# Two pairs' gate products computed beside the first token half, 19 pairs in place of 18, and another order in the first out stage

## The reference

```
for l in range(2):
    h = rms_norm(x, norm_gains[l, 0]);  z = h @ w_in[l]
    y_main = pool_mixer(...) if l == 0 else dilated_mixer(...)
    y = concatenate([y_main, memory_attn(...)]) @ w_out[l]      # "out"
    x = x + rms_norm(y, norm_gains[l, 1])
    h = rms_norm(x, norm_gains[l, 2])
    gu = h @ w_gate_up[l]                                       # "ffn", "st"
    y = (silu(gu[..., :2816]) * gu[..., 2816:]) @ w_down[l]     # "down"
    x = x + rms_norm(y, norm_gains[l, 3])
```

## Time and profile before

| what | before |
|---|---|
| median of three runs | 2039.13 us (2037.52 to 2039.89) |
| profiled execution, its own time | 2038.86 us |
| its span in the profile | 2037.2 us |
| mean granted clock of PE | 0.996 |
| PE busy | 1989.5 us, 98% |
| DVE busy | 1429.8 us, 70% |
| ACT busy | 894.0 us, 44% |
| POOL busy | 315.4 us, 15% |

### The profile page before, as it was taken

The page is one execution under the profiler, slowest core; times in us unless marked ns, Lnnn a source line. Parts: engine busy times, 40 slices in busy tenths (PEclk is TensorE's granted clock), DMA queues, the critical chain, the costliest instruction groups (busy, mean ns, idle before and its releaser), DMA issues.

```text
span 2037.2 us, 25039 instructions
## 1 busy us (share of the span) xinstructions
PE 1989.5 (98%) x9470; PEld 1597.3 (78%) x9470; DVE 1429.8 (70%) x1861; ACT 894.0 (44%) x1481; POOL 315.4 (15%) x177
## 2 busy tenths in 40 slices
PE   8999999999999999999999999999999999999997
PEld 6776878888888878888777776688788888888886
DVE  6567686576788875666445467677789988875665
ACT  6446353445545354343444456836522222234341
POOL 3645000111211000000000001210224323300001
PEclk9999999999999999999999999999999999999999
DMA  5228841456688877666222222152256644476644
GB/s 178 101 73 301 301 140 47 160 207 217 231 295 306 299 263 242 209 236 229 83 83 83 83 67 59 43 179 85 96 196 230 226 177 165 174 294 248 221 153 162
DMA packets 122199, 363.64 MB, mean 178 GB/s; under 512 B 11616, under 2 KB 13024, under 8 KB 116832
## 3 DMA queue, kind: packets, MB, share of 16 engines
q1 hardware_dynamic: 105616, 331.89, 46.2%
q10 hardware_dynamic: 16464, 30.15, 4.3%
HBM read 241.28 MB, written 114.43 MB: 175 GB/s over the span
## 4 chain that ended last, share of the span: by engine, by line
PE 46%; DVE 4%; issue 2%; ACT 2%; DMA 2%; POOL 0%; SPq 0%; POOLq 0%; ACTq 0%; DVEq 0%
PE PS L1013 5%; PE PS L1014 5%; PE PS L1015 5%; PE PS L750 5%; PE PS L755 5%; PE PS L751 5%; PE PS L1031 3%; PE PS L1032 3%; PE PS L1033 3%; PE PSC L886 2%; PE PTR L916 2%; PE PX L903 2%; DMA inner<-TP 1%; DVE SS L1884 0%; DVE CL L2138 0%
## 5 line engine op out<-in xcount | busy, mean ns | idle before, releaser
L1031 PE MATMUL PS<-RP,DH 128*128 128x512 f32 x616 | 240.6, 391 | 3.0 <-DVE RP L2320 3.0
L1033 PE MATMUL PS<-RP,DL 128*128 128x512 f32 x616 | 239.8, 389 | 0.0
L1032 PE MATMUL PS<-RP,DH 128*128 128x512 f32 x616 | 239.7, 389 | 0.0
L1013 PE MATMUL PS<-BHT,SH 128*128 128x512 f32 x576 | 224.1, 389 | 0.0
L1014 PE MATMUL PS<-BLT,SH 128*128 128x512 f32 x576 | 224.1, 389 | 0.0
L1015 PE MATMUL PS<-BHT,SL 128*128 128x512 f32 x576 | 224.1, 389 | 0.0
L2771 POOL TENSOR_TENSOR WL<-WR,WH 128x1024 fp32r<-128x1024 f32 (+2 forms) x40 | 84.1, 2117 | 677.0 <-ACT WH L1178 669.5
L1013 PE MATMUL PS<-BH,SH 128*128 128x512 f32 x432 | 168.3, 389 | 1.6 <-DVE TP L2168 0.9
L1015 PE MATMUL PS<-BH,SL 128*128 128x512 f32 x432 | 168.1, 389 | 0.0
L1014 PE MATMUL PS<-BL,SH 128*128 128x512 f32 x432 | 168.1, 389 | 0.0
L1031 PEld LDWEIGHTS PS<-RP,DH 128*128 128x128 f32 x616 | 115.6, 188 | 28.0 <-DVE RP L2320 4.1
(11 more groups left out here) (349 smaller groups left out, 4602.5 us busy)
## 6 DMA issues: line engine op xcount, KB each, us to landing
SR<-in_wst SPq DMA_DIRECT2D x36, 1024.0 KB, 4.8
ZS<-in_wdn SPq DMA_DIRECT2D x32, 704.0 KB, 6.1
s_keep<-ZS SPq DMA_DIRECT2D x32, 704.0 KB, 4.7
DR<-s_keep SPq DMA_DIRECT2D x32, 704.0 KB, 5.3
inner<-TP SPq DMA_DIRECT2D x36, 512.0 KB, 4.4
WR<-in_w SPq DMA_DIRECT2D x35, 512.0 KB, 6.1
DR<-in_wdn SPq DMA_DIRECT2D x24, 704.0 KB, 5.3
RR<-t_keep SPq DMA_DIRECT2D x16, 1024.0 KB, 5.2
```

The source lines that it names most:

```text
L1013: MM(BANK[bank], SH[b][:, w, c], BH[t][:, k, :], start=(k == 0), stop=False)
L1031: MM(bank, wh[:, i, :], rh, start=(i == 0), stop=False)
L1032: MM(bank, wh[:, i, :], rl, start=False, stop=False)
L1033: ins = MM(bank, wl[:, i, :], rh, start=False, stop=(i == KD - 1))
```

## The change

NHT goes from 4 to 3, so one tile more of each layer is a pair (19 in place of 18). A new kind of job, "early", computes products 0 and 2 of the first two pairs (24 matmuls each, two banks) right after the first plain tile's jobs of the first token half. ACT copies the first product (`early_copy`), DVE adds the second to it (`early_add`); both go to DRAM (early_keep) and come back when the pair runs, which then has five products. EARLY lies in the area of T4, so T4 is written after the stores, and product 5 alone waits for the low part of T4. In the out stage of layer 0 the column and row sums of x move from k steps 4 and 6 of job m = 5 to steps 0 and 2; ACT's output copies of y 4 and 5 stand earlier; each of the first half's stores of x has a semaphore of its own. The slots and banks of the plain jobs follow; slots of the pairs are now counted from the first pair, and `down_slot` is as before.

```diff
-NHT = 4
+NHT = 3
 NPAIR = NF - NHT
+NEARLY = 2
...
+        run = [Job("ffn", l, (0, j), halves=(0,), tag=0) for j in range(2)]
+        run += [Job("early", l, f, halves=(0,)) for f in range(NHT, NHT + NEARLY)]
+        run += [Job("ffn", l, (f, j), halves=(0,), tag=0) for f in range(1, NHT) for j in range(2)]
+        for n, o in enumerate(run):
+            o.slot = n if l else wide(n)
+        slot_of = {o.i: o.slot for o in run}
+        jobs += run
+        jobs += [Job("ffn", l, (f, j), halves=(1,), tag=1, slot=slot_of[f, j], share=("ffn", l, (f, j), 0))
+                 for f in range(NHT) for j in range(2)]
+        jobs += [Job("st", l, f, slot=(f - NHT + l) % 2) for f in range(NHT, NF)]
...
+    if o.name == "early":
+        if o.l:
+            return ((5, 6), (0, 1))[o.i - NHT]
+        return 2 * (n % 2), 2 * (n % 2) + 1
     if o.name == "ffn" and o.l == 1:
-        return ((2 * o.i[0] + o.i[1]) % 4,)
...
+                    if early and n in (0, 2):
+                        continue
+                    if n < 4 or early and n in (4, 6):
                         if bank in PS_WAIT[j]:
                             s, v = PS_WAIT[j][bank]
                             pe.wait_ge(named[s], v)
                     else:
...
+                    if (f, n) == (NHT, 5):
+                        pe.wait_ge(t_lo, 4 * l + 4)
...
-                              5: {4: [("col", s_x, 0)], 6: [("row", s_x, 0)]}}
+                              5: {0: [("col", s_x, 0)], 2: [("row", s_x, 0)]}}
...
+                    early_places = {NHT: {0: [("col", s_x, 0)], 4: [("row", s_x, 0)]}}
...
+                        if (h, f) == (0, 0):
+                            for e in range(NHT, NHT + NEARLY):
+                                early_job(l, e, after_k(early_places[e]) if e in early_places else None)
...
+                if q == 3:
+                    act.wait_ge(early_kept, early_kept_all(l))
...
-                            ("r", 6), ("y", 3), ("r", 7), ("n", 0), ("w", 0), ("h", 0), ("y", 4), ("h", 1), ("w", 1),
-                            ("h", 2), ("h", 3), ("y", 5), ("w", 2), ("h", 4), ("h", 5), ("w", 3), ("y", 6), ("h", 6),
+                            ("r", 6), ("y", 3), ("r", 7), ("y", 4), ("n", 0), ("w", 0), ("h", 0), ("h", 1), ("y", 5),
+                            ("w", 1), ("h", 2), ("h", 3), ("w", 2), ("h", 4), ("h", 5), ("w", 3), ("y", 6), ("h", 6),
...
+            def early_add(l, i):
+
+                q = NPAIR * l + i
+                dve.wait_ge(p1_done, q + 1)
+                V.tensor_tensor(EARLY_TILES[:, i, 1, :], EARLY_TILES[:, i, 0, :],
+                                BANK[banks(J[("early", l, NHT + i, None)])[1]], ALU.add).then_inc(c11_done, 1)
...
                 t_low(l, 2)
-                t_low(l, 3)
+                if l == 0:
+                    t_low(l, 3)
+                    st_add(q0)
                 product(l, 1, 1)
-                if l:
-                    gate_scaled(2, 1)
-                else:
-                    st_add(q0)
                 st_raw_lo(q0)
-                product(l, 2, 1)
                 st_sum_lo(q0)
                 if l:
-                    gate_scaled(3, 1)
-                product(l, 3, 1)
+                    t_low(l, 3)
+                    gate_scaled(2, 1)
+                product(l, 2, 1)
                 dn = [J[("down", l, n, None)] for n in range(NDN)]
                 for f in range(NHT, NF - 1):
                     q = q0 + f - NHT
                     if f > NHT:
...
-                if PREV[j] is not None:
-                    sp.wait_ge(mm_done, PREV[j] + 1)
+                sp.wait_ge(mm_done, (J[("ffn", l, (1, 1), 1)] if f == NHT + 1 else PREV[j]) + 1)
                 sp.dma_start(SR[pair_slot(q)][:, 0:4, :], w_st[q].rearrange("p (b n) -> p b n", b=4)) \
-                    .then_inc(st_loaded[f % 2], 16)
+                    .then_inc(st_loaded[q % 2], 16)
+
...
+            def early_first_back(l, i):
+
+                if i:
+                    sp.wait_ge(u2_done, NPAIR * l + i)
+                else:
+                    sp.wait_ge(early_kept, early_kept_all(l))
+                    sp.wait_ge(mm_done, J[("ffn", l, (1, 1), 1)] + 1)
+                sp.dma_start(SCR[0][:, :], early_keep[:, i, 0, :]).then_inc(early_first, 16)
...
+                keep_half(l, 0, 0)
+                for i in range(NEARLY):
+                    keep_early(l, i)
+                for f in range(1, NHT):
                     keep_half(l, f, 0)
                 load_pair(l, NHT)
                 keep_half(l, 0, 1)
+                load_pair(l, NHT + 1)
+                early_first_back(l, 0)
+                early_gate_back(l, 0)
                 keep_half(l, 1, 1)
                 keep_half(l, 2, 1)
-                load_pair(l, NHT + 1)
```

More of the change, by code:

```diff
@@ L83, in weight_rows @@
         rows += [("ffn", l, (f, j)) for f in range(NHT) for j in range(2)]
+        rows += [("early", l, f) for f in range(NHT, NHT + NEARLY)]
     return rows
@@ L158, in on_dve @@
 def on_dve(o):
-    return o.name in ("ffn", "down") or (o.name, o.l, o.tag) == ("in", 0, None) and o.i >= NMT
+    return o.name in ("ffn", "early", "down") or (o.name, o.l, o.tag) == ("in", 0, None) and o.i >= NMT
 def presplit(o):
@@ L275 @@
             READ_OUT[_n, product_bank(_q - 1, _p)] = (PRODUCT_READ[_p], _q)
+        continue
+    if _job.name == "early":
+        for _p, _b in zip((0, 2), banks(_n)):
+            READ_OUT[_n, _b] = (PRODUCT_READ[_p], NPAIR * _job.l + _job.i - NHT + 1)
         continue
@@ L1016, in pair, with early_job @@
                     if n < 6:
-                        ins.then_inc(st_mm, 1)
+                        ins.then_inc(st_mm, 2 if early and n in (1, 3) else 1)
                     else:
                         ins.then_inc(mm_done, 1)
+            def early_job(l, f, hook=None):
+                j = J[("early", l, f, None)]
+                wh, wl = hi(j), lo(j)
+                begin(j)
+                for k in range(KT):
+                    bank, c = BANK[banks(j)[k // 4]], k % 4
+                    MM(bank, wh[:, k, :], bh(0, k), start=(c == 0), stop=False)
+                    MM(bank, wh[:, k, :], bl(0, k), start=False, stop=False)
+                    ins = MM(bank, wl[:, k, :], bh(0, k), start=False, stop=(c == 3))
+                    if k == KT - 1:
+                        ins.then_inc(mm_done, 1)
+                    if hook is not None:
+                        hook(2 * k + 1)
             def down(l, n, hook=None):
@@ L1437, in gate, with early_copy @@
                     A(T[1][:, HALF[h]], PS[j % 2][:, HALF[h]], ACT.Silu).then_inc(silu_done, 1)
+            def early_copy(l, i):
+                j = J[("early", l, NHT + i, None)]
+                act.wait_ge(mm_done, j + 1)
+                A(EARLY_TILES[:, i, 0, :], BANK[banks(j)[0]], ACT.Copy).then_inc(p1_done, 1)
             def t_split(l, q):
                 act.wait_ge(t_ready, 4 * l + q + 1)
+                if q == 3:
+                    act.wait_ge(early_kept, early_kept_all(l))
                 t = ("T1", "T3", "T2", "T4")[q]
@@ L1445, in st_raw_hi @@
             def st_raw_hi(q):
+                a = A22 if is_early(q) else A11
                 act.wait_ge(*st_seen(q))
-                A(SH[pair_slot(q)][:, A11:S3, :], SR[pair_slot(q)][:, A11:S3, :], ACT.Copy).then_inc(st_hi, 1)
+                if q % NPAIR == 1:
+                    act.wait_ge(mm_done, J[("ffn", q // NPAIR, (NHT - 1, 1), 1)] + 1)
+                A(SH[pair_slot(q)][:, a:S3, :], SR[pair_slot(q)][:, a:S3, :], ACT.Copy).then_inc(st_hi, 1)
             def st_sum_hi(q):
@@ L1576, in sub_layer @@
                 r = 2 * l + 1
-                ffn = [J[("ffn", l, (f, i), 0)] for f in range(NHT) for i in range(2)]
+                ffn = list(range(J["ffn", l, (0, 0), 0], J["ffn", l, (0, 0), 1]))
                 act.wait_ge(c_lo, 30 if l else 6)
@@ L2473, in sub_layer @@
                     normed(r, 1, range(4))
+                    product(l, 1, 0)
+                    normed(r, 1, range(4, KT))
                     product(l, 2, 0)
-                    normed(r, 1, range(4, KT))
-                    product(l, 3, 0)
                 else:
@@ L2506, in sub_layer @@
                         accumulate(s_y, 1, k)
-                    gate_scaled(1, 0)
-                    product(l, 1, 0)
+                    early_add(l, 0)
                     weight_lo(ffn[6])
                     invert(s_y, 1)
+                    early_add(l, 1)
                     weight_lo(ffn[7])
@@ L3153, in pack_weights @@
         else:
-            f, j = i
+            f, j = i if name == "ffn" else (i, 0)
             w = inp["w_gate_up"][l][:, j * DFF + P * f:j * DFF + P * (f + 1)]
```

139 lines of the change are left out of this document (89 added, 50 removed).

## The result

The changed kernel takes 2097.8 us (median of 4 runs, 2094.0 to 2102.1), the kernel before 2038.9 (2037.5 to 2039.9, 4 runs): a ratio of 1.0295 with a 95% interval of 1.0283 to 1.0307, 59 us slower. The profiled execution took 2094.0 us, the fastest of the four; against that of before it is +55.1 us, the spans +55.0.

A forecast was written before the change was run, and what follows sets the result against it. PE, busy 98% of the span, was taken to bound the kernel. Matmuls' -5.5 us and +55.5 of waits (-5.1 + 21.6 + 16.1 + 17.4 = +50.0) gave 2089 us, range 2068 to 2103.

The forecast's parts named there:

- 2077 - 6 = 2071: Low end: layer 1's entry into the pairs covered (2077), transfers 3 us faster at each hand-over; the prediction wrote 2068.
- The hand-overs: Pairs to down jobs: first down weights load only at the last pair's end; +21.6 us layer 0, +17.4 layer 1.
- what need not be waited for: Hand-overs: products already done shorten the old offsets, by 1.3 us in layer 1 and 1.9 in layer 0.
- the row's 5.2: Hand-overs: a profile row's 5.2 us from a down weight's issue to ACT, kept over the page's estimated 3.7.
- Layer 0 up to the end of the pairs: Layer 0 before the hand-over: fewer matmuls and two old stalls gone, short pairs' stalls added; -5.1 us.
- The second early job: Layer 1, first token half: waits 3.0 us for the first plain tile's product, plus 1.6 for the clock; +4.6 us.
- Into the pairs: Layer 1: two plain jobs go, pairs hold more products, DVE sets the first pair's start; +11.5 us.
- some ten: Layer 1's entry: PE stands still some ten us, the first pair's first product waiting for the last gate_scaled.
- the counts were as read: Rival: waits are for earlier work than read; 2050 or 2033 us; 3%.
- layer 1's entry was not covered: Rival: gate_scaled runs where PE needs it, so 10.6 us and the clock's 1.6 come back; 2077 us, 15%.
- the transfers at the hand-overs were not 3 us faster: Rival: transfers go faster while PE is idle, 3 us off each hand-over; 2083 us, no separate chance given.
- the old offsets held almost in full: Rival: old hand-over offsets hold in full, 2 us more each, and the clock stays low longer; 2099 us, 20%.

The follow-up runs named there:

- four kernels: Down slots and product banks repaired on the changed kernel: 2048.7 us; slots only: 2063.3; banks only: 2087.5; down slots swapped in the kernel before: 2076.8.
- The out stage alone: The kernel before with only the first out stage changed (places of the sums, ACT's order, semaphores of x): 2036.8 us, ratio 0.9995.
- three repairs of layer 1's entry: Last gate_scaled first on the changed kernel: 2093.0 us; early jobs' banks on the slots-and-product-banks repair: 2048.9; DVE's low parts later, on all bank repairs: 2041.8.
- S: The changed kernel with down-weight slots and the pairs' product banks repaired: 2048.7 us, ratio 1.0056.
- the one with layer 0 alone: The change in layer 0 only, with all repairs; layer 1 keeps four plain tiles and 18 pairs as in the kernel before: 2035.9 us, ratio 0.9995.

## Why the prediction was right

It said 2089, 2068 to 2103; 2097.8 was measured. The range holds it, and the mechanisms are those of the forecast but for one that it lacks. The lower end of the range, 2068, is not what its terms give (2077 - 6 = 2071); nothing hangs on that. By its own steps, against the profiled executions (+50.0 forecast, +55.0 in the spans):

- *The hand-overs* were forecast at +21.6 and +17.4, their stalls at 22.2 and 16.5. The stalls were 23.8 and 17.4. The cost from layer 0's pairs' end to its norm behind the down jobs (the wait at 941.76, before at 923.90) is 17.9 + 4.8 = 22.7, that of layer 1 18.8. The mechanism, the releasers and the bank's share in layer 0 are shown by four kernels: both edits take it away, either makes part of it, and the slots alone make it in the kernel before. Mis-sized is the deduction for "what need not be waited for": I took 1.3 and 1.9 off the old offsets and 0.4 and 0.2 came. SP issued RR00 1.04 us behind DR where it was 2.72 before, 1.7 us sooner, but ACT had it at +9.7 (709.90) in place of +10.1 (1800.29), only 0.4 sooner, and c21 came 0.4 sooner too. RR02 (713.59) waited as before for stores and ZX loads ahead of it. In both stretches the DMA engines were busy nine tenths of the time, the last three figures being PE's clock, their share and GB/s, before and after, with ACT's row of before ahead of them:

```profile
1800.29 1.92 ACT L1481 ACTIVATE RP<-RR 128x2048 fp32r<-128x2048 f32 x1 [3.43 <-DMA RR<-inner]
```

```profile
1790.20:1802.20 12.00, 12.00 (x54) 9.94 (x54) 10.46 (x12) 4.84 (x5) 0.00 (x0) 1.00 0.90 323
```

```profile
700.20:714.20 14.00, 0.00 (x1) 0.00 (x0) 4.58 (x4) 4.55 (x3) 0.00 (x0) 0.64 0.92 327
```

So an earlier issue may only have queued; no run varies the traffic, and this cause stays open. The first weight itself reached ACT 4.2 us after its issue (704.46 against 700.24) and 4.15 in layer 1, 1 us sooner than the row's 5.2. The fit of the Trainium skill ("DMA: Bandwidth & Descriptors", section "Anatomy of one DMA — SWDGE (gpsimd) path"), by analogy an estimated 3.7 us, is nearer to it than the row. But the hand-overs were not 1 to 2 us shorter, as was drawn from it; they came out 1.1 and 1.4 us longer than the sum by the row.

- *Layer 0 up to the end of the pairs*: -4.8 against -5.1. The closeness is luck: the eleven kernels of this document with the changed layer 0 reached that point between 698.95 and 703.50 in their profiled executions. The out stage alone gave 2.0 (703.07), which is within that spread too.
- *The second early job*: its stall was 3.00 us, as forecast. The half clock behind it did not come in this execution, and part of the 3.0 was absorbed: DVE came to `t_make` 66.5 us after layer 1's first plain job, before 64.3, so 2.3 was passed on, not 4.6.
- *Into the pairs*: forecast +11.5. DVE's list took 30.5 us, forecast 31.4:

```profile
1457.51 6.22 DVE L2275 TENSOR_TENSOR TFT<-YOA 128x2048 f32<-128x2048 f32 x2
...
1480.12 0.68 DVE L2299 TENSOR_TENSOR SL<-SR,SH 128x512 fp32r<-128x512 f32 x1
...
1487.28 0.68 DVE L2243 TENSOR_TENSOR TP<-PS,RSTD 128x512 f32<-128x512 f32 x1
```

I had counted 1.0 too much for the raw low part, which has 512 columns in a pair with early products, as the order already showed; the 5.1 us charged for two sets of POOL adds came whole. PE stood still for 9.8 us, forecast "some ten", but in two stalls: 3.82 at 1474.01, before a plain job and for a product of a plain tile, and 6.02 before the first pair. So only the latter was released by the last `gate_scaled`, and a repair of that step alone could not get the ten back. The third pair's stall is 2.02, forecast 2.0. Pairs: 357.2 us against 342.8, +14.4, where 8.2 + 1.6 + 2.0 = 11.8 was forecast: the low clock came behind more than one stall (10 matmuls in the 4 us behind 1488.1 and 10 behind 1519.7, where full clock gives 17 to 18). Early job and entry together: 15.5 against 16.1.

- *Not in the prediction*: the 4.64 us before layer 1's first out job, in place of 2.35 close by in the kernel before; with its clock +2.8 us. The step "the slots and banks of the plain jobs follow" was read for the FFN alone; that 33 in place of 34 jobs turns the banks of the next mixing part was missed.
- The rest, from +55.0 of the profiled executions to +58.9 of the medians, is run to run (below).

The rivals: SP issued DR at the end of the last pair, so the counts were as read; layer 1's entry was not covered; the transfers at the hand-overs were not 3 us faster, and the old offsets held almost in full.

## What to carry to other kernels

When one unit is added to a ring of two or a count of jobs changes by an odd number, list every slot, bank and buffer whose index is taken modulo something, also in the stages behind: here three such turns (down slots, product banks, alternating banks) cost some 52 us, a ratio of 1.0295 against 1.0040, in a change that saved 5.5 us of matmuls. A first load of the next stage belongs into the region that is free one step before the last. And where another engine's serial list ends a stretch, work taken from PE there is not gained: in this kernel three repairs of layer 1's entry moved the wait and left its FFN at 444.4 us, and only the four plain tiles brought it back to 439.1.

## What was not expected of the hardware

The low clock is no fixed price. Behind the same stall of 3.00 us before the second early job, windows of the changed kernel and of S show:

```profile
1411.80:1415.80 4.00, 3.93 (x17) 3.30 (x18) 3.64 (x5) 2.02 (x5) 0.00 (x0) 1.00 0.19 70
```

```profile
1388.50:1392.50 4.00, 3.94 (x12) 3.17 (x13) 3.63 (x5) 2.01 (x5) 0.00 (x0) 0.64 0.19 70
```

17 matmuls at full clock in one, 12 in the other, where the granted clock was 0.64 in the mean of the 4 us, between the levels of 1.2 and 2.4 GHz. Behind the 23.8 us of the first hand-over it was

```profile
723.90:727.90 4.00, 3.88 (x9) 3.13 (x10) 3.30 (x6) 1.33 (x2) 0.00 (x0) 0.50 1.04 417
```

and full from 728 on: a stall of 24 us was followed by no more low clock (9 matmuls) than one of 2.7 us before. Behind the 17.4 us of the second it lasted a little longer (0.50 in the first 4 us, 0.82 in the next). Executions of one kernel differ along with it: the changed kernel ran from 2094.0 us at a mean clock of 0.982 to 2102.1 at 0.979, the one with layer 0 alone from 2032.1 at 0.998 to 2040.9 at 0.995. That spread, of which the clock may not be all, hides gains of 1 to 4 us that the parts of a profile show.
